# Two feed-forward matmuls merged into one of 512 columns, with one PSUM bank for each half of a slot

## The chip, the cores and the metric

The kernel runs on one core of a Trainium2 chip. The metric is the device time of one execution in microseconds (us). TensorE multiplies matrices into PSUM (8 banks of 128 x 512 float32), VectorE, ScalarE and GpSimd work on tiles in SBUF (GpSimd does not touch PSUM here), and the queue of SyncE starts the loads. In the rows the engines are called PE (matmuls), PEld (its weight loads), DVE (VectorE), ACT (ScalarE), POOL (GpSimd) and SPq.

## What is computed

A trunk of two layers over 256 tokens of width 1024. Each layer is a feed-forward, a token mixer of three branches, and another feed-forward:

```python
def _swiglu(h, w_in, w_out):
    gate, up = jnp.split(h @ w_in, 2, axis=-1)
    return (jax.nn.silu(gate) * up) @ w_out

for l in range(DEPTH):                      # 2
    mod = (c_act @ ada_w[l] + ada_b[l]).reshape(bsz, 3, 3, D_MODEL)
    h = _modulated_norm(x, norm_g[l, 0], mod[:, 0, 0], mod[:, 0, 1])
    x = x + MACARON_WEIGHT * mod[:, 0, 2][:, None, :] * _swiglu(h, ffn1_w_in[l], ffn1_w_out[l])
    ...                                     # token mixer
    h = _modulated_norm(x, norm_g[l, 2], mod[:, 2, 0], mod[:, 2, 1])
    x = x + MACARON_WEIGHT * mod[:, 2, 2][:, None, :] * _swiglu(h, ffn2_w_in[l], ffn2_w_out[l])
```

w_in is 1024 x 5632 (2816 gate and 2816 up columns), w_out 2816 x 1024, all float32.

## The kernel before

All weights stream through SBUF in slots of 128 x 2048, 100 slots a layer, four raw buffers and two rounded ones. Activations lie transposed: features on the partitions, the 256 tokens along the columns. Each product is made of three matmuls in a reduced float32 format: ScalarE rounds the raw weights (round_w, L561 to L568, tile wh), VectorE subtracts to get the remainder (split, L873 to L884, tile wl), and h is held as h_hi and h_lo in the same way. mm3 (L1406) then issues high weights by h_hi, high weights by h_lo, low weights by h_hi, 256 columns each, all added up in one place of a bank.

The first half of a feed-forward has 22 slots (KF, numbered j). A slot holds 128 gate and 128 up columns for all eight 128-row blocks of h. TensorE (ffn, L1489) does the gate half into columns 0 to 255 of bank j % 4 and the up half into columns 256 to 511 of the same bank (in_tile, L1423), 24 matmuls each. Slot 0 goes block by block as the norm delivers h (first_slot, L1412). At the start of slot j TensorE waits for hf of slot j - 4 (L1494).

When a slot's matmuls are done (w_used), ScalarE rounds the weights of slot j + 2 and takes the Silu of the gate half from PSUM (L602 to L607). VectorE splits slot j + 2 (L930), multiplies the up half in PSUM by the Silu into hf (L934), and then does one piece of the adaLN products (ada, L945 to L962): two instructions over 128 x 512, written ada below, the first of each group of four pieces a TENSOR_SCALAR. GpSimd turns hf into hid_hi (L1324) and hid_lo (L1326) for the second half of the feed-forward. Every fourth slot TensorE sums up a finished group of four ada pieces with four small matmuls (ada_sum, L1474 to L1481), issued behind slots 4, 8, 12, 16 and 20 of the first feed-forward of a layer and behind slots 8, 12, 16 and 20 of the second; the last piece it waits for is the one that VectorE does in the slot before. In the second feed-forward VectorE has ada pieces in slots 4 to 19 only.

The second half of the feed-forward (11 slots, row_slot, L1434) gathers its outputs in the four banks of OUT_BANKS (L151). Each engine works through its own queue in the order of the program; engines meet at semaphores whose counts are given per layer (PER_LAYER, L127), some with a start value (BEFORE, L149).

Of the kernel before, what the change touches and what calls it, by code (L numbers as in the profile page):

```python
# [29 lines left out]
P = 128  # L30
# [72 lines left out]
def shape_constants():  # L103
# [34 lines left out]
    "u_ready": 4, "gn_sub": 1, "gn_rinv": 1, "ya_final": 1, "ya_lo": 1, "mod_done":  # L138
    1, "br_used": 12, "merged": 4, "mg_lo": 4, "hid_ready": 44, "pb_zero": 1, "sb_min": 3,
    "shift_d": 12, "kk0": 1, "X_ready": 10, "vec_rows": 1, "w_used": 100,  # L140
# [9 lines left out]

OUT_BANKS = ((4, 5, 6, 2), (4, 5, 6, 7), (4, 5, 6, 2))  # L151
BR_BANKS = (0, 4, 0)
# [8 lines left out]
def hybrid_trunk(nc, a, per_layer, tally):  # L161
    out_dram = a["out"]
    ctx = ExitStack()
    with ctx:
# [24 lines left out]
        phase("h_gap", 64)  # L189
        hh = sb("h_hi", [P, KD, T], F32R)  # L190
        hl = sb("h_lo", [P, KD, T], F32R)
        scr = sb("scr", [P, KD, T])
# [52 lines left out]
        sil = v3(at_("sil", 2 * T), 2)  # L245
        hf = v3(at_("hf", 2 * T), 2)

        yh = v3(at_("y_hi", 9 * T, F32R, 0), 9)
# [69 lines left out]
        def bank(b):  # L318
            return PS[:, b, :]
# [240 lines left out]
        def _(act):  # L560
# [37 lines left out]
            def ffn(l, f):  # L598
                s0, s1 = (FFN1_IN, FFN1_OUT) if f == 0 else (FFN2_IN, FFN2_OUT)
                for s, o in steps(act, s0, KF):  # L600
                    j = s - s0
                    round_w(s + 2, o, l)  # L602
                    act.wait_ge(*at("w_used", s + 1 + o(4), l))

                    act.wait_ge(*at("hf_ready", f * KF + j - 1 + o(4), l))
                    nc.scalar.activation(sil[:, j % 2, :], PS[:, j % 4, 0:T], ACT.Silu)\
                        .then_inc(*one("sil_ready"))  # L607
                for s, o in steps(act, s1, 11, peel=1, tail=2):
                    if s < s1 + 9 or (s == s1 + 9 and f == 0):
                        round_w(s + 2, o, l)  # L610
# [259 lines left out]
        def _(dve):  # L870
# [55 lines left out]
            def ffn(l, f):  # L926
                s0, s1 = (FFN1_IN, FFN1_OUT) if f == 0 else (FFN2_IN, FFN2_OUT)
                for s, o in steps(dve, s0, KF, *((0, 0), (4, 2))[f]):
                    j = s - s0
                    split(s + 2, o, l)  # L930
                    dve.wait_ge(*at("sil_ready", f * KF + j + 1 + o(4), l))

                    dve.wait_ge(*at("hid_ready", f * KF + j - 1 + o(4), l))
                    V.tensor_tensor(hf[:, j % 2, :], PS[:, j % 4, T:2 * T], sil[:, j % 2, :], ALU.mult)\  # L934
                        .then_inc(*one("hf_ready"))
                    if f == 0 or 4 <= j < 20:
                        ada((16, 60)[f] + j, o, l)
                for s, o in steps(dve, s1, 11, peel=1, tail=2):
                    j = s - s1
                    if j < 9:  # L940
                        split(s + 2, o, l)
                    if 1 <= j <= 8:
                        ada((37, 79)[f] + j, o, l)
# [35 lines left out]

            for name in ("w_split", "hf_ready"):  # L980
                dve.sem_inc(sem(name), BEFORE[name])
            V.memset(epsb[:, :], EPS)
# [329 lines left out]
        def _(pool):  # L1312
            G = nc.gpsimd

            def ffn(l, f):
                s0 = FFN1_IN if f == 0 else FFN2_IN
                for s, o in steps(pool, s0, KF):
                    j = s - s0
                    pool.wait_ge(*at("hf_ready", f * KF + j + 1 + o(4), l))
                    dh = hidh[:, bass.ds(o(4) + j, 1), :].rearrange("p a b -> p (a b)")  # L1320
                    dl = hidl[:, bass.ds(o(4) + j, 1), :].rearrange("p a b -> p (a b)")

                    pool.sem_inc(sem("pool_on"), 1)
                    G.tensor_copy(dh, hf[:, j % 2, :])  # L1324
                    pool.drain()
                    G.tensor_tensor(dl, hf[:, j % 2, :], dh.bitcast(F32), ALU.subtract).then_inc(*one("hid_ready"))  # L1326

            pool.sem_inc(sem("hid_ready"), BEFORE["hid_ready"])

            r6 = slice(NOPE, P)  # L1330
# [72 lines left out]
        def _(pe):  # L1403
# [8 lines left out]
            def first_slot(s, b, h0, l):  # L1412
# [8 lines left out]
                return ins  # L1421

            def in_tile(s, half, b, col, n=P):  # L1423

                for k in range(KD):
                    w0 = (half * KD + k) * n
                    last = mm3(PS[0:n, b, col:col + T], (s % 2, slice(w0, w0 + n)), hh[:, k, :], hl[:, k, :],
                               k == 0, k == KD - 1)
                return last
# [59 lines left out]
            def ffn(l, f):  # L1489
                s0, s1 = (FFN1_IN, FFN1_OUT) if f == 0 else (FFN2_IN, FFN2_OUT)  # L1490
                for s, o in steps(pe, s0, KF, peel=(2, 6)[f]):
                    j = s - s0

                    pe.wait_ge(*at("hf_ready", f * KF + j - 3 + o(4), l))  # L1494
                    if j == 0:
                        ins = first_slot(s, 0, f * 2 * KD, l)
                    for half in range(2) if j else ():
                        split_ready(s, half, o, l)
                        ins = in_tile(s, half, j % 4, half * T)
                    ins.then_inc(*one("w_used"))  # L1500
# [4 lines left out]
                for s, o in steps(pe, s1, 11, *((1, 2), (2, 1))[f]):  # L1505
                    j = s - s1
                    pe.wait_ge(*at("hid_ready", f * KF + 2 * j + 2 + o(8), l))
                    if s == s1:

                        pe.wait_ge(*at("hid_ready", f * KF + 19, l))  # L1510

# [481 lines left out]
```

## Time and profile before

| | us |
|---|---|
| median of 3 runs | 1542.92 |
| lowest and highest | 1537.63, 1545.36 |
| the profiled execution | 1541.46 |
| its span, first to last instruction | 1539.7 |

The profiled execution is one of its own beside the three timed runs; all durations come from it. Its time stands 1.8 us over its span. A timeline row gives the start in us from the span's start, the duration in us, the engine, the line, the operation, what it writes and reads with their shapes, how many were merged into the row (x2), and in brackets how long the engine had been idle and what released it. TensorE's matmuls overlap one another: their pace is read from start to start, not from their durations.

### The profile page before, as it was taken

To read this page: it belongs to the slowest core of one execution; us is meant where nothing else is said; L and a number is where in the kernel's file an instruction comes from. 1 tells how busy PE (TensorE), PEld (TensorE's weight loads), DVE (VectorE), ACT (ScalarE), POOL (GpSimd) and SP (SyncE) were. 2 spreads that over 40 slices of the span, in tenths; PEclk is the share of its full clock that TensorE was granted. 3 is DMA by queue.
4 is the path that set the end of the run, shared out by engine and by line. 5 is a ranking of instruction groups with operands and counts; after the bars stand their busy time and mean duration, and the time that the engine had idled before them with its cause. 6 is when DMAs were issued, how large, how long until landed. Compare 5 with 4: busy or idle time off the path is not lost.

```text
span 1539.7 us, 31567 instructions
## 1 busy us (share of the span) xinstructions
PE 1401.4 (91%) x13297; PEld 1354.0 (88%) x13297; DVE 1009.5 (66%) x1327; ACT 652.2 (42%) x933; POOL 214.7 (14%) x250
## 2 busy tenths in 40 slices
PE   3699998978989998999989999897888999899997
PEld 3699998977779998999989999897777999899997
DVE  5777767656645776676677776765665468667655
ACT  2433434464533435334354333437373243543432
POOL 2133200021030000232003230002102000023200
PEclk9799999998999999999999999998999999999998
DMA  7998875923501856997669896792331095599860
GB/s 266 304 275 267 294 258 153 243 59 84 136 3 40 278 167 183 264 267 266 220 190 289 262 298 234 211 246 56 109 110 30 3 289 174 158 268 269 278 216 30
DMA packets 352798, 298.23 MB, mean 194 GB/s; under 512 B 19735, under 2 KB 295216, under 8 KB 352688
## 3 DMA queue, kind: packets, MB, share of 16 engines
q1 hardware_dynamic: 352688, 296.70, 64.5%
q8 instruction: 77, 1.26, 0.3%
q14 instruction: 33, 0.27, 0.1%
HBM read 295.61 MB, written 1.05 MB: 193 GB/s over the span
## 4 chain that ended last, share of the span: by engine, by line
PE 78%; DVE 10%; ACT 6%; DVEq 2%; issue 2%; DMA 2%; ACTq 1%; SPq 0%
PE PS L1408 21%; PE PS L1410 21%; PE PS L1409 21%; DVE ada_acc L961 3%; PE PS L1479 3%; ACT wh L567 2%; DVE wl L877 2%; PE PS L1825 2%; PE PS L1470 1%; DMA raw<-in_mix_w_in 1%; DVE PS L890 1%; DMA x_rows<-in_x 1%; PE PS L1816 1%; DVEq L948 1%; DVE scr L905 0%
## 5 line engine op out<-in xcount | busy, mean ns | idle before, releaser
L1408 PE MATMUL PS<-h_hi,wh 128*128 128x256 f32 x2256 | 645.4, 286 | 45.4 <-DVE h_lo L899 28.2
L567 ACT ACTIVATE wh<-raw 128x1024 fp32r<-128x1024 f32 (+1 forms) x400 | 396.0, 1038 | 607.9 <-PE PS L1410 583.0
L877 DVE TENSOR_TENSOR wl<-raw,wh 128x1024 fp32r<-128x1024 f32 (+1 forms) x400 | 473.6, 1225 | 270.2 <-ACT wh L567 270.2
L1409 PE MATMUL PS<-h_lo,wh 128*128 128x256 f32 x2256 | 637.8, 283 | 0.0
L1410 PE MATMUL PS<-h_hi,wl 128*128 128x256 f32 x2256 | 637.5, 283 | 0.0
L1408 PEld LDWEIGHTS PS<-h_hi,wh 128*128 128x128 f32 x2256 | 436.0, 193 | 51.3 <-issue 44.4
L1409 PEld LDWEIGHTS PS<-h_lo,wh 128*128 128x128 f32 x2256 | 437.1, 194 | 0.1
L1410 PEld LDWEIGHTS PS<-h_hi,wl 128*128 128x128 f32 x2256 | 436.6, 194 | 0.0
L961 DVE SCALAR_TENSOR_TENSOR ada_acc<-ada_w_ring,cact,ada_acc 128x512 f32<-128x512 f32 x280 | 219.4, 784 | 24.5 <-issue 1.8
L1408 PE MATMUL PS<-hid_hi,wh 128*128 (+1 forms) x704 | 197.7, 281 | 0.2
L1409 PE MATMUL PS<-hid_lo,wh 128*128 (+1 forms) x704 | 197.0, 280 | 0.0
L1410 PE MATMUL PS<-hid_hi,wl 128*128 (+1 forms) x704 | 197.0, 280 | 0.0
L1324 POOL CAST hid_hi<-hf 128x256 fp32r<-128x256 f32 x88 | 64.4, 732 | 728.3 <-DVE hf L934 728.3
L1409 PEld LDWEIGHTS PS<-hid_lo,wh 128*128 128x128 f32 x704 | 133.2, 189 | 0.0
L1410 PEld LDWEIGHTS PS<-hid_hi,wl 128*128 128x128 f32 x704 | 133.2, 189 | 0.0
L1408 PEld LDWEIGHTS PS<-hid_hi,wh 128*128 128x128 f32 x704 | 132.4, 188 | 0.3 <-issue 0.2
L1326 POOL TENSOR_TENSOR hid_lo<-hf,hid_hi 128x256 fp32r<-128x256 f32 x88 | 80.6, 916 | 12.7 <-issue 0.2
L1479 PEld LDWEIGHTS PS<-cst,ada_acc 128*128 128x128 f32 x320 | 41.3, 201 | 25.1 <-DVE ada_acc L961 17.6
L1479 PE MATMUL PS<-cst,ada_acc 128*128 128x1 f32 x320 | 43.0, 255 | 20.0 <-DVE ada_acc L961 19.6
L1383 POOL TENSOR_TENSOR rw_m<-scr 128x256 f32<-128x256 f32 x24 | 22.2, 944 | 158.4 <-ACT scr L659 86.9
L957 DVE TENSOR_SCALAR ada_acc<-ada_w_ring,cact 128x512 f32<-128x512 f32 x40 | 23.4, 585 | 30.2 <-PE PS L1479 16.9
L1398 POOL TENSOR_TENSOR A_X<-A_T,cst 128x384 f32<-128x384 f32 x20 | 23.4, 1172 | 135.1 <-DVE A_T L1189 109.1
(285 smaller groups left out, 1391.4 us busy)
## 6 DMA issues: line engine op xcount, KB each, us to landing
raw<-in_ffn_w_in SPq DMA_DIRECT2D x176, 512.0 KB, 5.4
ada_w_ring<-in_ada_w SPq DMA_DIRECT2D x160, 512.0 KB, 5.1
raw<-in_mix_w_in SPq DMA_DIRECT2D x90, 512.0 KB, 5.9
raw<-in_ffn_w_out SPq DMA_DIRECT2D x44, 1024.0 KB, 5.7
raw<-in_branch_w SPq DMA_DIRECT2D x8, 1024.0 KB, 8.2
raw<-in_mix_w_out SPq DMA_DIRECT2D x8, 1024.0 KB, 4.9
raw<-in_mix_w_in SPq DMA_DIRECT2D x2, 1024.0 KB, 7.5
w_mla<-in_mla_w_uq SPq DMA_DIRECT2D x4, 288.0 KB, 5.2
```

The costliest lines, as they stand in the source:

```text
L567: nc.scalar.activation(wh[:, s % 2, h * n:(h + 1) * n], raw[:, s % 4, h * n:(h + 1) * n], ACT.Copy).then_inc(*one("w_hi"))
L877: V.tensor_tensor(wl[:, s % 2, h * n:(h + 1) * n], raw[:, s % 4, h * n:(h + 1) * n], wh[:, s % 2, h * n:(h + 1) * n].bitcast(F32), ALU.sub ...
L957: V.tensor_scalar(acc[:, :], w, cc, None, ALU.mult)
L961: last = V.scalar_tensor_tensor(acc[:, :], w, cc, acc[:, :], ALU.mult, ALU.add)
L1324: G.tensor_copy(dh, hf[:, j % 2, :])
L1326: G.tensor_tensor(dl, hf[:, j % 2, :], dh.bitcast(F32), ALU.subtract).then_inc(*one("hid_ready"))
L1398: G.tensor_tensor(X[tt], AT[tt], chunk_mask(LEVELS[b]), ALU.mult).then_inc(*one("X_ready"))
L1408: M(out, wh[(slice(None),) + wsl], rhs_h, start=start, stop=False, skip_group_check=True)
L1409: M(out, wh[(slice(None),) + wsl], rhs_l, start=False, stop=False, skip_group_check=True)
L1410: return M(out, wl[(slice(None),) + wsl], rhs_h, start=False, stop=stop, skip_group_check=True)
L1479: ins = M(PS[:, 7, bass.ds(o(4) + col + i, 1)], acc[:, i * P:(i + 1) * P], onecol, start=True, stop=True)
L1825: ins = M(PS[half(q), b, o:o + 64], lhs[half(q), par, c, :], rhs[half(q), par, c, :], start=True, stop=True)
```

## The change

In the first half of both feed-forwards h_hi and h_lo now lie side by side for each block (tile h_both, of which hh and hl are views). The high weights meet both in one matmul of 512 columns, which fills a bank: columns 0 to 255 hold high by high, 256 to 511 high by low. The low weights meet h_hi in a second matmul of 256 columns into columns 0 to 255. Gate and up halves of a slot get a bank each, 2 * (j % 2) and the one after it. So TensorE waits at slot j for hf of slot j - 2.

ScalarE copies columns 256 to 511 of both banks to SBUF (gu), VectorE adds them to columns 0 to 255 (gu_sum), ScalarE takes the Silu of the gate sum from SBUF, and GpSimd, in place of VectorE, multiplies it by the up sum into hf, ahead of the two instructions it had. The second halves use bank 1 in place of bank 2.

```diff
-OUT_BANKS = ((4, 5, 6, 2), (4, 5, 6, 7), (4, 5, 6, 2))
+OUT_BANKS = ((4, 5, 6, 1), (4, 5, 6, 7), (4, 5, 6, 1))
...
-        hh = sb("h_hi", [P, KD, T], F32R)
-        hl = sb("h_lo", [P, KD, T], F32R)
+        both = sb("h_both", [P, KD, 2, T], F32R)
+        hh, hl = both[:, :, 0, :], both[:, :, 1, :]
...
+        gu = at_("gate_up", 4 * T)[:, :].rearrange("p (a b n) -> p a b n", a=2, b=2)
+        gu_sum = at_("gate_up_sum", 4 * T)[:, :].rearrange("p (a b n) -> p a b n", a=2, b=2)
...
# ScalarE, ffn
-                    nc.scalar.activation(sil[:, j % 2, :], PS[:, j % 4, 0:T], ACT.Silu)\
+                    for i in range(2):
+                        nc.scalar.activation(gu[:, j % 2, i, :], PS[:, 2 * (j % 2) + i, T:2 * T], ACT.Copy)\
+                            .then_inc(*one("gu_low"))
+                    act.wait_ge(*at("gu_ready", 2 * (f * KF + j) + 1, l))
+                    nc.scalar.activation(sil[:, j % 2, :], gu_sum[:, j % 2, 0, :], ACT.Silu)\
                         .then_inc(*one("sil_ready"))
...
# VectorE, ffn
                     split(s + 2, o, l)
-                    dve.wait_ge(*at("sil_ready", f * KF + j + 1 + o(4), l))
-
-                    dve.wait_ge(*at("hid_ready", f * KF + j - 1 + o(4), l))
-                    V.tensor_tensor(hf[:, j % 2, :], PS[:, j % 4, T:2 * T], sil[:, j % 2, :], ALU.mult)\
-                        .then_inc(*one("hf_ready"))
+                    dve.wait_ge(*at("hf_ready", f * KF + j - 1, l))
+                    for i in range(2):
+                        dve.wait_ge(*at("gu_low", 2 * (f * KF + j) + i + 1, l))
+                        V.tensor_tensor(gu_sum[:, j % 2, i, :], PS[:, 2 * (j % 2) + i, 0:T], gu[:, j % 2, i, :], ALU.add)\
+                            .then_inc(*one("gu_ready"))
...
# GpSimd, ffn
-                    pool.wait_ge(*at("hf_ready", f * KF + j + 1 + o(4), l))
+                    pool.wait_ge(*at("sil_ready", f * KF + j + 1, l))
+                    pool.wait_ge(*at("gu_ready", 2 * (f * KF + j) + 2, l))
...
+                    G.tensor_tensor(hf[:, j % 2, :], gu_sum[:, j % 2, 1, :], sil[:, j % 2, :], ALU.mult)\
+                        .then_inc(*one("hf_ready"))
+                    pool.drain()
                     G.tensor_copy(dh, hf[:, j % 2, :])
...
# TensorE
+            def both_halves(s, half, k, b, col, first, last):
+
+                w = (slice(None), s % 2, slice(col, col + P))
+                M(bank(b), wh[w], both[:, k, :, :].rearrange("p a b -> p (a b)"), start=first, stop=False,
+                  skip_group_check=True)
+                return M(PS[:, b, 0:T], wl[w], hh[:, k, :], start=False, stop=last, skip_group_check=True)
+
+            def wide_tile(s, half, b):
+                for k in range(KD):
+                    ins = both_halves(s, half, k, b, (half * KD + k) * P, k == 0, k == KD - 1)
+                return ins
...
-                    pe.wait_ge(*at("hf_ready", f * KF + j - 3 + o(4), l))
+                    pe.wait_ge(*at("hf_ready", f * KF + j - 1 + o(4), l))
                     if j == 0:
-                        ins = first_slot(s, 0, f * 2 * KD, l)
+                        ins = wide_first(s, f * 2 * KD, l)
                     for half in range(2) if j else ():
                         split_ready(s, half, o, l)
-                        ins = in_tile(s, half, j % 4, half * T)
+                        ins = wide_tile(s, half, 2 * (j % 2) + half)
...
-                        pe.wait_ge(*at("hid_ready", f * KF + 19, l))
+                        pe.wait_ge(*at("hf_ready", f * KF + 21, l))
```

wide_first does for slot 0 what wide_tile does, block by block as h comes. The start value of hf_ready is now set by GpSimd.

## Rows read from the trace of the kernel before

**Rows 1.** The page: busy time by engine; the chain that ended last, by engine.

```profile
PE 1401.4 (91%) x13297; PEld 1354.0 (88%) x13297; DVE 1009.5 (66%) x1327; ACT 652.2 (42%) x933; POOL 214.7 (14%) x250
...
PE 78%; DVE 10%; ACT 6%; DVEq 2%; issue 2%; DMA 2%; ACTq 1%; SPq 0%
```

**Rows 2.** Windows, one slot: busy us per engine, clock, DMA share, GB/s.

```profile
148.50:154.00 5.50, 5.50 (x49) 5.34 (x48) 4.26 (x6) 2.28 (x3) 2.02 (x3) 1.00 0.96 285
```

**Rows 3.** Timeline, TensorE: first and last of 192 matmuls (four slots).

```profile
132.01 0.36 PE L1408 MATMUL PS<-h_hi,wh 128*128 128x256 f32 x1
...
153.76 0.28 PE L1410 MATMUL PS<-h_hi,wl 128*128 128x256 f32 x1
```

**Rows 4.** Timeline, TensorE: first and last of 48 matmuls of 128 columns.

```profile
281.36 0.22 PE L1462 MATMUL PS<-wh,h_hi 128*128 128x128 f32 x1
...
286.55 0.28 PE L1464 MATMUL PS<-wl,h_hi 128*128 128x128 f32 x1
```

**Rows 5.** Timeline of one slot's steps: start us, us, engine, line.

```profile
148.69 2.01 ACT L567 ACTIVATE wh<-raw 128x1024 fp32r<-128x1024 f32 x2 [3.16 <-PE PS L1410]
150.61 0.36 ACT L606 ACTIVATE sil<-PS 128x256 f32<-128x256 f32 x1
...
149.79 2.36 DVE L877 TENSOR_TENSOR wl<-raw,wh 128x1024 fp32r<-128x1024 f32 x2 [1.07 <-ACT wh L567]
152.07 0.42 DVE L934 TENSOR_TENSOR hf<-PS,sil 128x256 f32<-128x256 f32 x1
152.58 1.58 DVE L961 SCALAR_TENSOR_TENSOR ada_acc<-ada_w_ring,cact,ada_acc 128x512 f32<-128x512 f32 x2
...
152.65 0.93 POOL L1324 CAST hid_hi<-hf 128x256 fp32r<-128x256 f32 x1 [3.34 <-DVE hf L934]
153.73 1.01 POOL L1326 TENSOR_TENSOR hid_lo<-hf,hid_hi 128x256 fp32r<-128x256 f32 x1
...
154.30 1.05 PE L1479 MATMUL PS<-cst,ada_acc 128*128 128x1 f32 x8 [0.26 <-DVE ada_acc L961]
155.21 0.36 PE L1408 MATMUL PS<-h_hi,wh 128*128 128x256 f32 x1
```

**Rows 6.** Timeline of the next slot (TENSOR_SCALAR first), and POOL beside an idle VectorE.

```profile
158.08 0.68 DVE L957 TENSOR_SCALAR ada_acc<-ada_w_ring,cact 128x512 f32<-128x512 f32 x1 [0.16 <-issue]
158.84 1.07 DVE L961 SCALAR_TENSOR_TENSOR ada_acc<-ada_w_ring,cact,ada_acc 128x512 f32<-128x512 f32 x1
...
158.08 0.40 POOL L1324 CAST hid_hi<-hf 128x256 fp32r<-128x256 f32 x1 [3.34 <-DVE hf L934]
158.63 0.74 POOL L1326 TENSOR_TENSOR hid_lo<-hf,hid_hi 128x256 fp32r<-128x256 f32 x1
...
612.13 0.73 POOL L1326 TENSOR_TENSOR hid_lo<-hf,hid_hi 128x256 fp32r<-128x256 f32 x1
```

**Rows 7.** Timeline: a weight split with POOL at work beside it.

```profile
319.77 3.43 DVE L877 TENSOR_TENSOR wl<-raw,wh 128x1024 fp32r<-128x1024 f32 x2
...
319.94 2.18 POOL L1376 TENSOR_TENSOR sb_z<-sb_z,cst 128x512 f32<-128x512 f32 x1 [1.66 <-DVE sb_s L1034]
```

**Rows 8.** Timeline, TensorE: where sums of the ada group start.

```profile
84.09 1.05 PE L1479 MATMUL PS<-cst,ada_acc 128*128 128x1 f32 x8 [0.27 <-DVE ada_acc L961]
...
107.90 1.05 PE L1479 MATMUL PS<-cst,ada_acc 128*128 128x1 f32 x8
...
131.10 1.05 PE L1479 MATMUL PS<-cst,ada_acc 128*128 128x1 f32 x8 [0.27 <-DVE ada_acc L961]
...
645.87 1.05 PE L1479 MATMUL PS<-cst,ada_acc 128*128 128x1 f32 x8 [0.26 <-DVE ada_acc L961]
```

**Rows 9.** Timeline, ScalarE: the first slot of the two feed-forwards of layer 0.

```profile
62.16 2.01 ACT L567 ACTIVATE wh<-raw 128x1024 fp32r<-128x1024 f32 x2 [4.28 <-PE PS L1410]
64.19 1.28 ACT L606 ACT_TABLE_LOAD   x1
...
602.19 2.01 ACT L567 ACTIVATE wh<-raw 128x1024 fp32r<-128x1024 f32 x2 [3.46 <-PE PS L1410]
```

More of the change, by code:

```diff
@@ L138 @@
     "u_ready": 4, "gn_sub": 1, "gn_rinv": 1, "ya_final": 1, "ya_lo": 1, "mod_done":
-    1, "br_used": 12, "merged": 4, "mg_lo": 4, "hid_ready": 44, "pb_zero": 1, "sb_min": 3,
+    1, "br_used": 12, "merged": 4, "mg_lo": 4, "hid_ready": 44, "gu_low": 88, "gu_ready": 88, "pb_zero": 1, "sb_min": 3,
     "shift_d": 12, "kk0": 1, "X_ready": 10, "vec_rows": 1, "w_used": 100,
@@ L977, in half_gate @@
                 return V.tensor_scalar(hgate[:, n, :], mod[:, (3 * n + 2) * KD:(3 * n + 3) * KD], w, None, ALU.mult)
-            for name in ("w_split", "hf_ready"):
-                dve.sem_inc(sem(name), BEFORE[name])
+            dve.sem_inc(sem("w_split"), BEFORE["w_split"])
             V.memset(epsb[:, :], EPS)
@@ L1328, in _ @@
             pool.sem_inc(sem("hid_ready"), BEFORE["hid_ready"])
+            pool.sem_inc(sem("hf_ready"), BEFORE["hf_ready"])
             r6 = slice(NOPE, P)
@@ L1421, in first_slot, with wide_first @@
                 return ins
+            def both_halves(s, half, k, b, col, first, last):
[7 more added lines that the diff above has]
+                return ins
+            def wide_first(s, h0, l):
+                split_ready(s, 1, still, l)
+                for k in range(KD):
+                    pe.wait_ge(*at("h_ready", h0 + k + 1, l))
+                    for half in range(2):
+                        ins = both_halves(s, half, k, half, (half * KD + k) * P, k == 0, k == KD - 1)
+                return ins
             def in_tile(s, half, b, col, n=P):
```

## The prediction, made before the change was run

> **What bounds the kernel now.** I read the page first: TensorE is busy 91% of the span and carries 78% of the chain that ended last [rows 1]. In a slot of a feed-forward's first half it works without a hole at granted clock 1.00, the 2.4 GHz level [rows 2]. So I asked what sets its pace. Four slots, 192 matmuls of 256 columns, start within 21.75 us, 113.3 ns apart but for the first step [rows 3]; a slot of 48 lasts L = 5.44 us. A matmul of 128 columns, half the streaming, follows its predecessor in 110.4 ns (5.19 us over 47 steps) [rows 4]. The pace hardly depends on the columns: what an instruction and its weight load cost each time sets it. That is where the change can win.
>
> Then I followed one slot through the other engines [rows 5]. Its matmuls end at E = 148.43: the next slot's last one starts at 153.76 [rows 3], plus 0.11, less 5.44. ScalarE's rounding starts at E + 0.26, VectorE's two splits end at E + 3.64 (152.07), hf runs to E + 4.06, the ada pair ends at E + 5.73 (154.16), and the ada sum starts on TensorE at E + 5.87 (154.30). The next slot's matmuls begin 0.91 later [rows 5] and lose another 0.09 on their first step, so 1.00. The ada sum is needed only every fourth slot, and there it, not TensorE, ends the wait: four slots take 3L + 5.87 + 1.00 = 23.19 us, and the trace has 131.10 to 154.30, 23.20 [rows 5, 8]. There is a longer kind, 84.09 to 107.90, 23.81 [rows 8], in which the matmuls are 117.8 ns apart (L = 5.65). Of the 14 such spans in the four feed-forwards, nine are short and five long: mean 23.41. GpSimd's result is not waited for today: a bank is used again four slots later.
>
> **Part 1, the matmuls.** Per slot, 16 triples of 256 columns become 16 pairs of 512 and 256. Columns are the same. The 256 part keeps its 113.3 ns. The wide part has no row: it can't stream under 2 x 106.7 = 213.3 ns at 2.4 GHz, and at worst costs two of today's, 226.6. I add to the column time what half the columns fail to save today, 113.3 - 110.4 = 2.9 ns [rows 3, 4], giving 216.2. L' = 16 x (216.2 + 113.3) = 5.27 us; bounds 16 x (213.3 + 110.4) = 5.18 and 5.44, or 5.65 at the long kind's pace. So at best 0.17 to 0.26 us of 5.44 are won in a slot, if nothing else is late.
>
> **Part 2, two banks a slot.** A slot now fills two of four banks, so TensorE waits at slot j for hf of slot j-2, where it waited for j-4. Everything from the end of slot n to hf(n) must fit in the one slot between. All of TensorE's next matmuls and weight loads are queued behind that wait. The steps, from E as above:
> - ScalarE: rounding as before, to about E + 2.2. Then two PSUM copies of 256 columns, 0.36 each by the Silu's row [rows 5], to about E + 2.9, under VectorE's splits: nothing, as long as the splits are later than that.
> - VectorE: splits to E + 3.64. First add 0.42 (the row of hf, same operands) to E + 4.06. Second add 0.42 to E + 4.48.
> - Silu from SBUF, from E + 4.09: 0.36, at most 0.5, beside the second add.
> - VectorE's ada pair starts 0.09 after its last PSUM step, GpSimd 0.16 after it [rows 5]. GpSimd now multiplies: two inputs, 256 columns, 0.73 to 0.74 us when VectorE is idle (the row of hid_lo) [rows 6].
>
> **Part 3, GpSimd beside VectorE.** In the rows the cast takes 0.40 us alone but 0.93 when the ada pair's first instruction started before it, and hid_lo 1.01 instead of 0.74 [rows 5, 6]. It ends 1.00 after that first instruction's start, so it was let in at 0.60. The other way round, an ada instruction that meets hid_lo already running takes 1.07, not 0.75 [rows 6]. They shut one another out. The Trainium skill, SBUF - State Buffer, section Who interferes with whom, has the same as a rule: whoever starts first holds a port pair they share, and the other is blocked for the whole instruction. It speaks against this change, which puts a third GpSimd instruction into this stretch; taken literally it would make the split below late by up to 0.74 rather than 0.40, some 6 us more.
>
> Priced from the rows: the first ada instruction starts at E + 4.57, the multiplication is let in at 5.17, ends at 5.91. TensorE starts 0.14 after its releaser [rows 5] and loses 0.09 on the first step: H = 6.1 us after E (5.6 where no ada pair blocks it, in the second feed-forwards' slots 0 to 3; 5.3 if it cost no more than a cast). H is over L' in each of these. The ada pair's second instruction meets the multiplication and ends 0.3 later; with the second add the ada sum moves from E + 5.87 to E + 6.59.
>
> After the multiplication come cast and hid_lo, to about E + 7.7 (today E + 6.3, 154.74). The next slot's split starts at E + L' + 1.36 = E + 6.6. Today it starts after GpSimd is done. From now on, where two slots follow without a stall, it meets hid_lo. A pair of splits with GpSimd beside it all the time took 3.43 instead of 2.36, against 2.2 us of GpSimd work and more [rows 5, 7]. For one 0.74 us instruction I take 0.40 (bounds 0 and 0.74). Then GpSimd itself is 0.40 later in that slot, and a third slot's split, though it comes after a stall (E + 6.10 + 1.36 = E + 7.5 against E + 8.1), meets it as well. So the ada sum, which hangs on such a slot, starts K = 6.99 after its E.
>
> **The sum.** Let a slot begin after an ada sum, at 0. The second begins at L' (two slots back was long ago), the third at L' + H, since it waits for hf of the first, which ended at L'. It ends at L' + H + L'. The sum hangs on its ada pair and starts K later (the fourth slot fits in between), and 1.00 after that the next slot begins. In all L' + H + L' + K + 1.00 = 10.54 + 6.10 + 6.99 + 1.00 = 24.63 us, where 23.41 stood. +1.22, fourteen times: +17.1.
> First feed-forward, slot 0 to its first sum: today 84.09 - 61.90 = 22.19 (61.90 is 62.16 less the 0.26) [rows 8, 9]. Now slot 0's Silu has a table load of 1.28 before it [rows 9], which the add holds back: hf(0) lets slot 2 start at 0.26 + 3.83 + 1.28 + 0.39 + 0.16 + 0.74 + 0.23 = 6.9. Slot 3 starts at 12.17, ends at 17.44, sum at 17.44 + 6.99 = 24.43. +2.24, twice: +4.5.
> Second feed-forward, eight slots to its first sum: today 645.87 - 601.93 = 43.94 [rows 8, 9]. Now slot 2 starts at 6.9, 4 at 12.17 + 5.6 = 17.8, 6 at 23.04 + 5.95 = 29.0, slot 7 at about 34.8, ends 40.1, sum at 47.1. +3.1, twice: +6.2.
> Last slot, 5.52 to 5.27, four times: -1.0.
> Everything else (norms, second halves, bank 1 in place of 2, the layout of h, at the first slot columns at the low clock) costs nothing: bank 1 was last read in slot 20, two slots before its new user. Total +26.8. The profiled execution took 1541.5, 1.5 under the median of 1542.9: 1541.5 + 26.8 = 1568.
>
> **The rivals.**
> (a) Nothing shuts out: the multiplication takes 0.74, splits aren't late, the table load comes ahead of the wait for the add. H = 5.6, K = 6.29; four slots 10.54 + 5.6 + 6.29 + 1.0 = 23.43, heads +0.9, last slots -1.0: 1542. For it: 0.73 in slots without ada [rows 6]. Against it: 0.93 and 1.01 wherever the ada pair runs [rows 5].
> (b) Half of it: the multiplication is blocked, the splits aren't late. K = 6.59: 24.23 for four slots, +11.5, heads +8.3, -1.0: 1560.
> (c) The wide matmul wins nothing (the change doesn't do what it says), with the stalls: L' = 5.44, four slots 24.97, +21.8, heads +12.8, -0.3: 1576. At 5.65, 1585.
> (d) Faster: GpSimd's path fits in a slot, H at most 5.2, and the wide matmul is at its bound, L' = 5.18. Then TensorE stalls at the ada sum alone: 3 x 5.18 + 6.29 + 1.0 = 22.83, -8.1; heads -3.5, last slots -1.4: 1528. The point is H = L': the multiplication would have to take 0.33 us or less, under the 0.40 of a cast [rows 6].
>
> **How the numbers follow.** The sum as it stands, with (b) as its weaker form: 0.62. (a) 0.15, (c) 0.13, (d) 0.08, the rest 0.02. Predicted 1568. The range leaves out (d) and what lies past (c): 1541 to 1580. About 0.5% is what a measurement of this kernel can tell from no change, 1535 to 1551: faster 0.08 (d), same 0.15 (a), slower 0.77.
>
> **What would show it.** In the changed trace: pairs of matmuls near 329 ns; TensorE idle 0.6 to 0.9 us at every second or third slot's start, released by GpSimd's hf, 1.6 at slot 2; hf on GpSimd over 1.2 us long beside the ada pair; the second ada instruction near 1.07; ada sums 24.6 apart; some split pairs near 2.8. If TensorE never waits for hf, or the sums are under 23.4 apart, the argument is wrong.

## The result and the profile after

| | before | after |
|---|---|---|
| median, us | 1542.95 (1537.63 to 1545.36, 4 runs) | 1576.54 (1574.55 to 1577.93, 4 runs) |
| the profiled execution (its span) | 1541.46 (1539.7) | 1577.93 (1576.1) |
| ratio to before, 95% interval | 1 | 1.0222 (1.0192 to 1.0251) |
| TensorE instructions of 128x1 to 128x512 | 13297 | 11889 |

The changed kernel is slower by 2.2%: 1568 was predicted, with 1541 to 1580 as the range. The time lies inside the range, 8.5 us above the forecast. The profiled executions differ by 36.5 us, from 1541.46 to 1577.93.

The page of the kernel after: busy time by engine, the chain by engine, and two groups (busy us, mean ns of one, idle time ahead of them with its releaser). The first two lines answer to [rows 1].

```profile
PE 1424.0 (90%) x11889; PEld 1298.8 (82%) x11889; DVE 1071.3 (68%) x1415; ACT 712.7 (45%) x1109; POOL 280.9 (18%) x338
...
PE 70%; DVE 12%; ACT 8%; issue 3%; DVEq 3%; DMA 2%; POOLq 1%; ACTq 1%; SPq 0%
...
L1437 PE MATMUL PS<-h_both,wh 128*128 128x512 f32 x1408 | 511.4, 405 | 24.4 <-DVE h_both L906 19.9
...
L1331 POOL TENSOR_TENSOR hf<-gate_up_sum,sil 128x256 f32<-128x256 f32 x88 | 89.6, 1018 | 688.3 <-ACT sil L613 688.3
```

TensorE runs 1408 matmuls fewer and is busy 23 us longer. Its share of the last chain falls from 78% to 70%; DVE, ACT and the queue of POOL take it over. So both were at work: the matmuls took no less time, and TensorE waits more.

The timeline of TensorE after: a whole stretch between two ada sums, against [rows 3, 5, 8]. "..." leaves out matmuls of the same pace. The last row is GpSimd's multiplication ahead of the first hole.

```profile
110.14 0.28 PE L1439 MATMUL PS<-h_both,wl 128*128 128x256 f32 x1
111.09 1.05 PE L1510 MATMUL PS<-cst,ada_acc 128*128 128x1 f32 x8 [0.67 <-DVE ada_acc L968]
112.00 0.48 PE L1437 MATMUL PS<-h_both,wh 128*128 128x512 f32 x1
...
117.37 0.40 PE L1437 MATMUL PS<-h_both,wh 128*128 128x512 f32 x1
...
117.72 0.40 PE L1437 MATMUL PS<-h_both,wh 128*128 128x512 f32 x1
...
123.26 0.28 PE L1439 MATMUL PS<-h_both,wl 128*128 128x256 f32 x1
123.68 0.50 PE L1437 MATMUL PS<-h_both,wh 128*128 128x512 f32 x1
...
129.30 0.28 PE L1439 MATMUL PS<-h_both,wl 128*128 128x256 f32 x1
129.69 0.50 PE L1437 MATMUL PS<-h_both,wh 128*128 128x512 f32 x1
...
136.27 0.27 PE L1510 MATMUL PS<-cst,ada_acc 128*128 128x1 f32 x1 [0.68 <-DVE ada_acc L968]
...
122.43 1.12 POOL L1331 TENSOR_TENSOR hf<-gate_up_sum,sil 128x256 f32<-128x256 f32 x1 [4.53 <-ACT sil L613]
```

Read it by starts. Inside a slot the pair repeats every 0.35 us (117.37 to 117.72), of which the wide matmul takes 0.234 and the narrow one 0.118. The next slot follows at once at 117.72. The third starts 0.42 after its predecessor's last matmul (123.26 to 123.68), the fourth 0.39 after (129.30 to 129.69), where 0.12 is the pace: holes of about 0.3 us, and the first step after each is 0.1 slower. These rows have no bracket, but hf is done at 123.55 (122.43 + 1.12), 0.13 before the first late start, about the 0.14 that TensorE keeps from its releaser in [rows 5]. From sum to sum it is 25.18 us. All 14 such spans of the four feed-forwards measure 25.17 to 25.22, where 23.20 and 23.81 stood [rows 8]: (25.19 - 23.41) x 14 = 24.9 of the 36.5 us.

The other engines in the same stretch, after, against [rows 5, 6] (timeline; the last slot before the sum at 111.09, whose steps begin at 104.50; E = 104.24).

```profile
104.50 2.01 ACT L570 ACTIVATE wh<-raw 128x1024 fp32r<-128x1024 f32 x2 [1.43 <-PE PS L1439]
...
105.60 2.70 DVE L884 TENSOR_TENSOR wl<-raw,wh 128x1024 fp32r<-128x1024 f32 x2 [0.66 <-ACT wh L570]
108.22 0.74 DVE L941 TENSOR_TENSOR gate_up_sum<-PS,gate_up 128x256 f32<-128x256 f32 x2
109.05 1.90 DVE L968 SCALAR_TENSOR_TENSOR ada_acc<-ada_w_ring,cact,ada_acc 128x512 f32<-128x512 f32 x2
...
105.34 0.74 POOL L1336 TENSOR_TENSOR hid_lo<-hf,hid_hi 128x256 fp32r<-128x256 f32 x1
109.28 1.12 POOL L1331 TENSOR_TENSOR hf<-gate_up_sum,sil 128x256 f32<-128x256 f32 x1 [3.20 <-ACT sil L613]
```

The split pair ends later because hid_lo of the slot before (105.34 to 106.08) runs beside it: 2.70 instead of 2.36. The ada pair takes 1.90 instead of 1.58, hf 1.12 where GpSimd took 0.73 for the like beside an idle VectorE [rows 6]. By its instructions hf takes 733 ns at least, 1117 in the median, 1125 at most.

### The profile page after: what moved, and what is told of

It is laid out like the page before. It is cut to its first block, busy times and chain, and to the rows that moved or that the text cites. A ratio compares the mean times of both kernels' runs of the same rounds, so it can differ in the third digit from the quotient of the medians.

```text
span 1576.1 us, 29191 instructions
## 1 busy us (share of the span) xinstructions
PE 1424.0 (90%) x11889; PEld 1298.8 (82%) x11889; DVE 1071.3 (68%) x1415; ACT 712.7 (45%) x1109; POOL 280.9 (18%) x338
## 4 chain that ended last, share of the span: by engine, by line
PE 70%; DVE 12%; ACT 8%; issue 3%; DVEq 3%; DMA 2%; POOLq 1%; ACTq 1%; SPq 0%
PE PS L1437 14%; PE PS L1419 12%; PE PS L1420 11%; PE PS L1421 11%; PE PS L1439 7%; ACT wh L570 4%; DVE ada_acc L968 3%; DVE wl L884 3%; PE PS L1510 2%; PE PS L1856 2%; DVEq L955 2%; PE PS L1501 1%; POOLq L1333 1%; DMA raw<-in_mix_w_in 1%; DVE PS L897 1%
## 5 line engine op out<-in xcount | busy, mean ns | idle before, releaser
L884 DVE TENSOR_TENSOR wl<-raw,wh 128x1024 fp32r<-128x1024 f32 (+1 forms) x400 | 493.8, 1274 | 243.3 <-ACT wh L570 243.3
L1437 PE MATMUL PS<-h_both,wh 128*128 128x512 f32 x1408 | 511.4, 405 | 24.4 <-DVE h_both L906 19.9
L1439 PE MATMUL PS<-h_both,wl 128*128 128x256 f32 x1408 | 398.1, 283 | 0.0
L1437 PEld LDWEIGHTS PS<-h_both,wh 128*128 128x128 f32 x1408 | 267.8, 190 | 101.5 <-issue 38.3
L1419 PE MATMUL PS<-h_both,wh 128*128 128x256 f32 x848 | 248.3, 293 | 25.4 <-DVE h_both L906 8.3
L1439 PEld LDWEIGHTS PS<-h_both,wl 128*128 128x128 f32 x1408 | 267.5, 190 | 0.0
L968 DVE SCALAR_TENSOR_TENSOR ada_acc<-ada_w_ring,cact,ada_acc 128x512 f32<-128x512 f32 x280 | 236.1, 843 | 23.4 <-issue 0.5
L1420 PE MATMUL PS<-h_both,wh 128*128 128x256 f32 x848 | 242.9, 286 | 0.0
L1421 PE MATMUL PS<-h_both,wl 128*128 128x256 f32 x848 | 242.7, 286 | 0.0
L1331 POOL TENSOR_TENSOR hf<-gate_up_sum,sil 128x256 f32<-128x256 f32 x88 | 89.6, 1018 | 688.3 <-ACT sil L613 688.3
L1419 PEld LDWEIGHTS PS<-h_both,wh 128*128 128x128 f32 x848 | 166.8, 197 | 30.0 <-issue 23.0
L1420 PEld LDWEIGHTS PS<-h_both,wh 128*128 128x128 f32 x848 | 167.5, 198 | 0.1
L1421 PEld LDWEIGHTS PS<-h_both,wl 128*128 128x128 f32 x848 | 166.5, 196 | 0.0
L613 ACT ACTIVATE sil<-gate_up_sum 128x256 f32<-128x256 f32 x88 | 36.8, 418 | 126.1 <-DVE gate_up_sum L941 126.1
```

The costliest lines, as they stand in the source:

```text
L613: nc.scalar.activation(sil[:, j % 2, :], gu_sum[:, j % 2, 0, :], ACT.Silu)\
L884: V.tensor_tensor(wl[:, s % 2, h * n:(h + 1) * n], raw[:, s % 4, h * n:(h + 1) * n], wh[:, s % 2, h * n:(h + 1) * n].bitcast(F32), ALU.sub ...
L968: last = V.scalar_tensor_tensor(acc[:, :], w, cc, acc[:, :], ALU.mult, ALU.add)
L1331: G.tensor_tensor(hf[:, j % 2, :], gu_sum[:, j % 2, 1, :], sil[:, j % 2, :], ALU.mult)\
L1419: M(out, wh[(slice(None),) + wsl], rhs_h, start=start, stop=False, skip_group_check=True)
L1420: M(out, wh[(slice(None),) + wsl], rhs_l, start=False, stop=False, skip_group_check=True)
```

## Experiments

Each kernel was timed beside the kernel before on one chip. The medians of before in the three series are 1542.74, 1540.84 and 1542.26 us; the ratios below are to those. "Sums" are the starts of successive ada sums on TensorE, 14 spans in a run.

**One wide matmul or two narrow ones.** The changed kernel, its 512-column matmul issued as two of 256, all else as changed:

```diff
-                M(bank(b), wh[w], both[:, k, :, :].rearrange("p a b -> p (a b)"), start=first, stop=False, ...)
+                M(PS[:, b, 0:T], wh[w], hh[:, k, :], start=first, stop=False, ...)
+                M(PS[:, b, T:2 * T], wh[w], hl[:, k, :], start=False, stop=False, ...)
```

> The changed kernel with its 512-column matmul issued as two of 256 columns (48 matmuls and weight loads a slot again, into the same banks); all else as changed. Theory 1: the wide matmul costs by its columns (234 ns, twice 117), the weight loads it saves were hidden anyway; then the time stays within 5 us of the changed kernel's 1577, the ada sums 25.2 us apart. Rival (the prediction's): every instruction with its load costs some 10 ns of its own; then a slot is 0.17 us longer and the kernel 8 us slower, 1585. Third: narrow matmuls get back to 113.3 ns in part of the slots, as in the kernel before; then it is faster by up to 8 us, 1569.

Measured: 1575.59 us (1572.80 to 1576.08), ratio 1.021 (1.0178 to 1.0243), sums 24.97 to 25.00 apart in 8 spans and 25.17 to 25.18 in 6. Timeline of TensorE, narrow kernel:

```profile
119.83 0.28 PE L1438 MATMUL PS<-h_both,wh 128*128 128x256 f32 x1
...
120.73 0.28 PE L1437 MATMUL PS<-h_both,wh 128*128 128x256 f32 x1
```

The rows shown are the first and the ninth matmul: eight steps in 0.90 us, 113 ns each, so that three take 0.34 against 0.35 for the wide pair. About half of the triples in these spans take 0.34, the others 0.35. The first theory holds, and in part the third: the wide matmul saves nothing; a 512-column matmul costs two of 256 at the slower of the two paces that before shows. The whole gain that the change was to pay with is absent.

**Multiplication back on VectorE.** Here hf is computed by VectorE from the sums, after the adds and ahead of the ada pair; GpSimd casts and subtracts as before (the waits that go with it are left out of the diff):

```diff
+                    V.tensor_tensor(hf[:, j % 2, :], gu_sum[:, j % 2, 1, :], sil[:, j % 2, :], ALU.mult)...
                     if f == 0 or 4 <= j < 20:
                         ada((16, 60)[f] + j, o, l)
...
-                    G.tensor_tensor(hf[:, j % 2, :], gu_sum[:, j % 2, 1, :], sil[:, j % 2, :], ALU.mult)...
```

> The changed kernel with the multiplication into hf moved back from GpSimd to VectorE, behind the two adds; GpSimd has its two instructions of before. Theory: GpSimd's blocked multiplication (1.12 us) is what makes hf later than a slot (6.0 to 6.3 us after the slot's end against 5.64), so with 0.42 us on VectorE hf is ready after about 5.3 us, TensorE doesn't wait for it, splits return to 2.36, the ada sum comes about 6.75 after its slot's end: 24.7 us between sums, 12 us faster in all, 1565. Rival: the matmuls alone make the loss and the stalls are covered by something else; then 1577 stays.

Measured: 1584.09 us (1581.38 to 1588.01), ratio 1.0276 (1.0241 to 1.031): 7.5 us above the changed kernel's median, where 12 us less or no change had been expected. The holes at the starts of slots are gone. Seven of the 14 spans are 24.89 to 25.02, the other seven 26.39 to 26.44. The windows around one of the latter (the sum starts at 108.68; busy us of each engine with the number of instructions, granted clock, DMA share, GB/s):

```profile
108.70:111.00 2.30, 2.30 (x16) 2.09 (x17) 2.28 (x2) 1.48 (x3) 0.42 (x1) 0.98 1.18 319
111.00:114.50 3.50, 3.50 (x13) 3.02 (x12) 3.09 (x6) 0.42 (x1) 1.13 (x2) 0.53 0.79 249
114.50:118.00 3.50, 3.50 (x22) 3.04 (x21) 0.08 (x1) 0.90 (x1) 0.00 (x0) 1.00 1.03 301
```

and two wide matmuls of the same stretch (timeline, TensorE):

```profile
111.20 0.63 PE L1437 MATMUL PS<-h_both,wh 128*128 128x512 f32 x1
...
111.84 0.63 PE L1437 MATMUL PS<-h_both,wh 128*128 128x512 f32 x1
```

TensorE stood still from its last matmul of the slot (107.26) to the sum, 1.42 us. Some 2.3 us after the sum's start the granted clock falls to 0.53 in the mean of a window, the 1.2 GHz level for most of it; the pair takes 0.64 us (111.20 to 111.84) instead of 0.35. Five such pairs cost 5 x 0.29 = 1.5 us, the difference of the two kinds of span. K is 6.96 here (E = 101.72), as late as in the changed kernel: three slots without a hole, 1.00 + 3 x 5.64 + 6.96 = 24.88, are all that moving the multiplication saves, 0.3 us of 25.19. TensorE comes to the sum earlier and waits longer, and the seven slow stretches cost more than the 14 x 0.3 us.

**A third pair of banks.** The changed kernel with pairs of banks taken in turn by j % 3 and TensorE waiting for hf of slot j-3 (TensorE's loop over the slots is written out for it, and the second halves go back to bank 2):

```diff
-                    pe.wait_ge(*at("hf_ready", f * KF + j - 1 + o(4), l))
+                    pe.wait_ge(*at("hf_ready", f * KF + j - 2 + o(4), l))
...
-                        ins = wide_tile(s, half, 2 * (j % 2) + half)
+                        ins = wide_tile(s, half, 2 * (j % 3) + half)
```

> The changed kernel with three pairs of banks instead of two (TensorE's loop over the slots written out), so that it waits for hf of slot j - 3; GpSimd's work stays. Theory: the stalls at slot starts (0.3 us each) and 1.3 us at slot 2 go, the ada sum still ends each four slots: 3 x 5.64 + 6.9 + 1.0 = 24.8 us between sums instead of 25.2, 10 us faster in all, 1567. Rival: the wait moves to the splits or the sum and nothing is won, 1577.

Measured: 1582.96 us (1580.99 to 1588.55), ratio 1.0258 (1.0226 to 1.0291), where 10 us less or no change had been expected. The pattern is that of the kernel before it: six spans of 24.90 to 24.92, eight of 26.41 to 26.47. With no stall at the slots, GpSimd's work and the splits lie on one another. Timeline of this kernel, VectorE, GpSimd, TensorE:

```profile
104.98 2.91 DVE L884 TENSOR_TENSOR wl<-raw,wh 128x1024 fp32r<-128x1024 f32 x2 [0.28 <-ACT wh L570]
...
105.10 1.71 POOL L1336 TENSOR_TENSOR hid_lo<-hf,hid_hi 128x256 fp32r<-128x256 f32 x1
...
109.16 0.28 PE L1439 MATMUL PS<-h_both,wl 128*128 128x256 f32 x1
110.59 1.05 PE L1510 MATMUL PS<-cst,ada_acc 128*128 128x1 f32 x8 [1.15 <-DVE ada_acc L968]
```

Two engines that meet cost each other 0.55 us (split) and 0.97 us (hid_lo) here. And the idle time ahead of the sum is 1.43 us again.

**Is it the idle time that lowers the clock?** The kernel with the multiplication on VectorE, and eight matmuls of 256 columns ahead of every ada sum, into a bank that nobody reads then; they are work that the reference doesn't ask for:

```diff
+                        for _ in range(8):
+                            M(PS[:, 6, 0:T], hh[:, 0, 0:P], hh[:, 0, :], start=True, stop=True)
                         ada_sum((3, 14)[f] + j // 4, l, o)
```

> a_dve with eight matmuls of 256 columns, whose result nobody reads, ahead of every ada sum, so that TensorE works through most of the 1.4 us that it waits there for VectorE. Theory: a_dve (1584) is slower than the changed kernel only because in about half of its spans the granted clock falls to half for some 3 us after this idle stretch (24.9 us between sums where it does not fall, 26.4 where it does); with the stretch filled all spans take 24.9 and the kernel 1584 - 9 x 1.5 = 1570. Rival: the clock falls for another reason; then 1584 and the spans of 26.4 stay.

Measured: 1573.27 us (1565.17 to 1575.98, 5 runs), ratio 1.021 (1.0175 to 1.0245). All 14 spans are 24.88 to 25.02. Timeline of TensorE and one window of this kernel:

```profile
109.14 1.12 PE L1534 MATMUL PS<-h_both 128*128 128x256 f32 x8
110.45 1.05 PE L1510 MATMUL PS<-cst,ada_acc 128*128 128x1 f32 x8 [0.19 <-DVE ada_acc L972]
...
111.00:114.50 3.50, 3.50 (x22) 3.09 (x22) 3.21 (x5) 1.37 (x4) 0.00 (x0) 1.00 0.90 274
```

Work that nobody needs makes the kernel faster, by the medians 10.8 us (1584.09 to 1573.27), about 7 x 1.5; by the ratios 0.0066, about 10 us. The clock stays at 1.00. The mean granted clock of the executions says the same: 0.951 to 0.959 in the four without the eight matmuls, 0.960 to 0.966 in the five with them. So the slow stretches came from TensorE standing still ahead of the sum.

**Taking the wait at the sum away.** The ada sum is moved into the middle of the next slot, after its first half, where the ada pair is long done:

```diff
                         ins = wide_tile(s, half, 2 * (j % 2) + half)
+                        if half == 0 and j % 4 == 1 and j >= (5, 9)[f]:
+                            ada_sum((3, 14)[f] + j // 4, l, o)
```

The old place is removed. The edit was made in the changed kernel, in the one with the third pair of banks, in the one with the multiplication on VectorE, and in the kernel before, the last with in_tile in place of wide_tile.

> The changed kernel with each ada sum issued between the halves of the next slot; the multiplication stays on GpSimd and the banks stay two pairs. Theory: the wait for the ada pair goes, the waits for hf stay: two slots take 5.64 + 6.1, four 23.5 to 24.1 us instead of 25.2, about 1560. Rival: only the wait for hf counts and the sum was hidden behind it; then 1577.

> Three pairs of banks and the ada sum between the halves: no wait of TensorE for hf of two slots back or for the ada pair; GpSimd still multiplies. Theory: what is left is VectorE and GpSimd shutting each other out (splits of 2.9 us instead of 2.36, ada pairs of 1.9 instead of 1.6), 5.7 to 5.8 us of VectorE a slot, 23.6 to 24.0 us in four, about 1552. Rival: with TensorE never idle they fit into 5.64 and the time is that of a_dve_mid or better.

> a_dve (multiplication on VectorE) with each ada sum issued between the halves of the next slot, so that TensorE has neither a wait for hf nor one for the ada pair, and no idle stretch after which its clock is lower. Theory: both losses of the changed kernel are these waits; four slots take 4 x 5.64 + 0.95 = 23.5 us, the whole about 1548 (the table load still delays slot 2). Rival: VectorE, with 2.4 + 0.75 + 0.43 + 1.6 us and the gaps between them in a slot of 5.64, becomes the bound, 24.2 us and 1558 or more.

> The kernel before with each ada sum of the feed-forwards' first halves issued between the two halves of the next slot instead of ahead of it. Theory: the sum's wait for VectorE's ada pair (0.43 us over the end of the slot) goes; four slots take 4 x 5.44 + 0.95 = 22.7 instead of 23.2, eighteen times: 8 us faster than before, 1535. Rival: VectorE's next group of ada pieces now waits for the later sum and gives it back, 1543.

| the sum in the middle, in | us, median | ratio (interval) | sums apart, us |
|---|---|---|---|
| the changed kernel | 1564.91 (1564.18 to 1572.30) | 1.0175 (1.0135 to 1.0216) | 24.61 to 24.65 |
| with three pairs of banks | 1546.99 (1541.41 to 1551.58) | 1.0040 (1.0018 to 1.0062) | 23.50 |
| with the multiplication on VectorE | 1545.17 (1539.66 to 1548.96) | 1.0030 (1.0012 to 1.0048) | 23.50 |
| the kernel before | 1542.34 (1533.83 to 1546.14) | 0.9996 (0.9975 to 1.0017) | 23.50 to 23.51 |

In the changed kernel the wait for hf remains, and costs more than was expected of it (1565, not 1560). Timeline of TensorE, starts of two successive slots:

```profile
95.93 0.28 PE L1439 MATMUL PS<-h_both,wl 128*128 128x256 f32 x1
96.34 0.49 PE L1437 MATMUL PS<-h_both,wh 128*128 128x512 f32 x1
...
101.97 0.28 PE L1439 MATMUL PS<-h_both,wl 128*128 128x256 f32 x1
102.36 0.49 PE L1437 MATMUL PS<-h_both,wh 128*128 128x512 f32 x1
```

A slot takes 6.02 us, 0.37 more than the 5.65 of its matmuls. The slot with the sum has 0.90 of its own and hides the wait: 3 x 6.02 + 5.65 + 0.90 = 24.61. With the wait for hf gone as well, in either way, the span is 4 x 5.65 + 0.90 = 23.50, TensorE has no hole in it, and 4 to 6 us over before are left. The two waits together are all the rest of the loss. The kernel with three pairs of banks had been expected to stay slower for its meetings of VectorE and GpSimd; they are still there (2.94 us for a split pair, up to 1.71 for hid_lo), and cost nothing in the spans once TensorE waits for neither. The timeline of TensorE in the kernel with the multiplication on VectorE, and in before with the sum moved (its first sum):

```profile
110.29 0.95 PE L1510 MATMUL PS<-cst,ada_acc 128*128 128x1 f32 x8
```

```profile
80.01 0.28 PE L1410 MATMUL PS<-h_hi,wl 128*128 128x256 f32 x1
...
83.41 0.28 PE L1410 MATMUL PS<-h_hi,wl 128*128 128x256 f32 x1
83.53 0.95 PE L1479 MATMUL PS<-cst,ada_acc 128*128 128x1 f32 x8
...
84.65 0.28 PE L1410 MATMUL PS<-h_hi,wl 128*128 128x256 f32 x1
...
86.77 0.28 PE L1410 MATMUL PS<-h_hi,wl 128*128 128x256 f32 x1
```

Neither row of the sum has a bracket: nothing is waited for. In before this wins nothing, because all matmuls of the 14 spans now run at the long pace of 117.8 ns: 4 x 5.65 + 0.90 = 23.5 in every span, where before had 23.20 in nine spans and 23.81 in five. The rival's 1543 came, but not by its mechanism: VectorE waits for the sums no longer than in before (15.5 us in the whole execution, 16.9 before). Nor is it enough to say that matmuls without a stop run at the long pace. In the rows above 30 steps from 80.01 to 83.41 take 113.3 ns each, as do all from 60.1 us on, without a stop; behind the sum, for which TensorE did not wait either, 18 steps from 84.65 to 86.77 take 117.8.

**Another way to shorten the wait of before.** The kernel before with the ada pair ahead of the split on VectorE:

```diff
+                    if f == 0 or 4 <= j < 20:
+                        ada((16, 60)[f] + j, o, l)
                     split(s + 2, o, l)
```

> The kernel before with VectorE's ada piece of each slot put ahead of its weight split, into the 1.07 us in which it waits for ScalarE, so that the ada sum never waits. Theory: four slots take 4 L + 0.95; at the pace of 113.3 ns a matmul that is 22.7 us instead of 23.4 on average and the kernel is 8 to 10 us faster, 1533. Rival: as in b_mid, matmuls that never stop at a sum run at 117.8 ns (L = 5.65), 23.5 us, and nothing is won, 1543.

Measured: 1542.46 us (1536.55 to 1552.65, 12 runs), ratio 1.0013 (0.999 to 1.0036), spans 23.50 to 23.51, all at the long pace. It ends where the moved sum did, as its rival said.

**What a narrow matmul costs.** The changed kernel with its 512 columns cut unequally, another cut in each feed-forward: 448+64, 384+128, 320+192 and four of 128. It was run once.

```diff
+                cuts[0] = ((448,), (384,), (320,), (128, 256, 384))[2 * l + f]
```

> The changed kernel with the 512-column matmul cut in another way in each of the four feed-forwards, all columns still computed: 448 + 64, then 384 + 128, then 320 + 192, then four of 128. Read from start to start inside a slot. Theory 1 (price by column, 0.458 ns each, with a floor of some 110 ns from the weight load): 205, 176 and 147 ns for 448, 384 and 320 columns, 110 for 64, 128 and 192. Rival (the prediction's term: 2.4 GHz column time and 2.9 ns a piece): 190, 163 and 136 ns. Theory 1 also says that the first three cuts cost a slot 16 x about 80 ns more than the wide matmul.

Timeline of TensorE, stretches of the four feed-forwards (a row x2 stands for the two pieces, a row x4 for the four):

```profile
99.68 0.40 PE L1442 MATMUL PS<-h_both,wh 128*128 128x448 f32 x2
99.92 0.36 PE L1445 MATMUL PS<-h_both,wl 128*128 128x256 f32 x1
100.11 0.40 PE L1442 MATMUL PS<-h_both,wh 128*128 128x448 f32 x2
...
639.79 0.40 PE L1442 MATMUL PS<-h_both,wh 128*128 128x384 f32 x2
...
640.19 0.39 PE L1442 MATMUL PS<-h_both,wh 128*128 128x384 f32 x2
...
859.70 0.40 PE L1442 MATMUL PS<-h_both,wh 128*128 128x320 f32 x2
859.94 0.30 PE L1445 MATMUL PS<-h_both,wl 128*128 128x256 f32 x1
...
860.84 0.40 PE L1442 MATMUL PS<-h_both,wh 128*128 128x320 f32 x2
...
1450.29 0.95 PE L1442 MATMUL PS<-h_both,wh 128*128 128x128 f32 x4
...
1451.36 0.95 PE L1442 MATMUL PS<-h_both,wh 128*128 128x128 f32 x4
```

The same 768 columns take 0.433, 0.403 and 0.380 us in the first three (the last is three rounds in 1.14 us, 859.70 to 860.84), against 0.353 in one wide and one narrow matmul: extra 80, 50 and 27 ns. Columns at the pace of the wide matmul cost 234.6 / 512 = 0.458 ns each, so 64, 128 and 192 columns would take 29, 59 and 88 ns; if none of them can take less than the 110.4 ns of [rows 4], the extras would be 81, 52 and 22. All three fit within 5 ns; the 80 ns that the expectation gave for every cut was its own slip. The rows also show where the time goes. From the first piece to the 256-column matmul it is 0.23 to 0.24 us, the price of 512 columns, whatever the cut; the lost time comes in the step behind that, 0.19 (99.92 to 100.11) where 0.12 is the pace. So the rival's 2.4 GHz column time falls, and what the small piece costs is a floor under its turn, not a price paid beside the columns: a matmul of 256 columns (117 ns of columns) is already above it. That the floor is the time of the weight load, as the expectation has it, no run shows. The fourth feed-forward, at 1.07 us, can't be read with the others, since it ran at the low clock; see the last section. The kernel took 1854.72 us.

## Why the prediction was right, and where it was not

- **L', the time of a slot's matmuls: the step that failed.** Predicted 5.27, with 5.44 and 5.65 as the upper bounds; measured 5.64 to 5.65, 16 pairs of 0.353 where the sign was 0.329. The prediction read from 110.4 ns for 128 columns beside 113.3 for 256 [rows 3, 4] that an instruction has a fixed price and that its columns are nearly free, and gave the wide matmul 213.3 + 2.9 ns. The runs show a floor of about 110 ns and a column price of 0.443 to 0.460 ns, which happen to meet near 256 columns. The wide matmul is all columns: 234.6 ns, not 216.2. This term alone is 2 x 0.37 = 0.74 us of a four-slot span. It is the mechanism of rival (c), which had a chance of 0.13. The number is right because the range reached as far as that rival; the gain that the change was to bring, 0.17 us a slot, did not come.
- **The same term by the Trainium skill.** The Trainium skill, TensorE: Matmul & The Clock Gate, section Wait — 56ns, not 53.3ns?, puts back-to-back matmuls at the full clock at columns / 2.4 GHz plus some 2.5 ns, which makes an estimate of 215.8 ns for 512 columns. The trace disagrees: 234 to 235 ns at granted clock 1.00; the measurement decides. The section does not say whether its matmuls had this number format and a weight load each, as these have. Its formula gives nearly the size that the prediction had formed from rows, and both were short by 18 to 19 ns.
- **H, the wait for hf: right.** Predicted 6.1 us from the end of slot n to a full-speed slot n+2; measured 123.68 - 117.73 = 5.95, plus 0.09 on the first step, 6.04. Since L' is longer than predicted, the hole is 0.3 us and not 0.6 to 0.9. The sign "hf over 1.2 us beside the ada pair" was a little high: 1.12.
- **K, from E to the ada sum: right.** Predicted 6.99; measured 111.09 - 104.24 = 6.85, where 5.87 stood. Its parts: the second add and the blocked ada pair, and the split behind hid_lo, 0.34 of the 0.40 taken. The rule of the Trainium skill, SBUF - State Buffer, section Who interferes with whom, taken literally, asked up to 0.74 for that split; the trace stays below it here: the two overlap for 0.48 us (105.60 to 106.08), and the split lost 0.34. With the third pair of banks, where they overlap by more, the split lost 0.55.
- **The span.** 1.00 + 5.64 + 6.04 + 5.64 + 6.85 = 25.17; measured 25.17 to 25.22; predicted 24.63. Two terms of -0.06 and -0.14 stand against +0.74. Over 14 spans the miss is 24.9 - 17.1 = 7.8 us, nearly all of the 9.7 us by which the profiled execution passed the sum of 26.8.
- **The heads (from the end of slot 0 to the first ada sum): right in sum, by luck, since two errors cancel.** 85.92 - 61.55 = 24.37 (predicted 24.43) and 655.24 - 608.25 = 46.99 (predicted 47.1). But the predicted idle time of 1.6 us at slot 2 isn't there: its first matmul starts at 67.31, 5.76 after the end of slot 0, not 6.9. The table load was predicted to stand behind the wait for the add. Timeline of ScalarE and VectorE in that slot, after:

```profile
64.38 1.28 ACT L613 ACT_TABLE_LOAD   x1
65.18 0.75 DVE L941 TENSOR_TENSOR gate_up_sum<-PS,gate_up 128x256 f32<-128x256 f32 x2
65.67 0.42 ACT L613 ACTIVATE sil<-gate_up_sum 128x256 f32<-128x256 f32 x1
```

  The load starts at 64.38, 0.80 before the add that the Silu waits for, and is over at 65.66, where the add was done by about 65.59. It costs 0.07 here. The longer L' gave back what this saved.
- **Last slots and the rest.** -1.0 was predicted for the four last slots, from the shorter L'; with 5.64 nothing is won. All that lies outside spans and heads changed by 36.5 - 24.9 - 2 x (2.18 + 3.05) = +1.1 us in sum, as +3.9 and -2.9 between single feed-forwards. It was not taken apart.
- **The rivals.** (a) falls: hf takes 1.12 where the ada pair runs, and the splits are late; only its third part, the table load ahead of the wait for the add, is what happened. (b) falls with the late splits. (d) needed hf under 0.33 us. (c) with its 5.44 gave 1576, and the median is 1576.5; but with the measured 5.64 it would have given nearly 1585. It was met by 5.64 together with a smaller H and K and no stall for the table load.
- **What each half of the change costs.** The matmul's width is worth nothing (narrow against wide, 1575.6 and 1576.5). The waits are worth nearly everything: with both gone the kernel is at 1545, 1547. What is left there, 4 to 6 us, is 0.3 to 0.4% and clear of noise. The pace of the matmuls is of that size: in before the 4 and 8 slots ahead of the first sums all run at 113.3 ns, so 24 slots are 5.65 instead of 5.44, 5.0 us, and the 14 spans are 23.50 instead of 23.41, 1.3 us. No run takes that pace away, so this is worked out, not shown.

No kernel of these is faster than the one before.

## What to carry to other kernels

Before fusing two matmuls into a wider one, find two widths in the trace and ask whether the narrower shows a floor or a price per instruction: only a price is saved by fusing, and a pace near the floor looks like one. When work is moved to a second engine to free the first, count the stretches in which the two now meet and the number of slots that the result may be late; and if a chain feeds TensorE at one point only, moving that point by half a slot takes the chain off the path, as long as the chain is late by less than that; here it was late by 6.85 - 5.64 = 1.2 us against half a slot of 2.8.

## What the runs showed of the hardware

- **Idle time and the clock.** In the kernel after, TensorE stands still 0.95 us (start of the last matmul to start of the sum, 110.14 to 111.09) before each ada sum, and in all 14 spans the clock stays at 1.00. After stops of 1.42 us, counted in the same way, the clock fell in 15 of 28 spans (7 of 14 with the multiplication on VectorE, 8 of 14 with three pairs of banks, there every second time within a feed-forward), for some 3 us, and in the stretch shown it began to fall only 2.2 us after the sum's start. With matmuls in the gap it never fell in them. What decides between the 15 and the 13 was not found.
- **A stream of 128-column matmuls at the low clock.** Two windows of the kernel with the unequal cuts, one over the last feed-forward's first half and one behind it:

```profile
1389.30:1774.90 385.60, 385.55 (x1807) 385.58 (x1808) 100.20 (x132) 68.67 (x116) 48.24 (x63) 0.50 0.30 87
1775.00:1780.00 5.00, 5.00 (x46) 5.00 (x45) 1.20 (x3) 1.41 (x3) 1.87 (x3) 1.00 0.63 210
```

  TensorE is busy almost without a hole (385.55 of 385.60 us), and the granted clock is 0.50, the 1.2 GHz level, from the start of the 128-column matmuls at 1389.35 to their end (their last round starts at 1770.72) and 3 us into the 256-column matmuls behind them; then it rises. A round of 768 columns took 1.07 us, of which 640 ns are the columns at 1.2 GHz. Ahead of the low level TensorE had stopped for 4.17 us. Over the first halves with the first three cuts the clock is 0.97 to 1.00, and the kernel after, with a stop of 4.16 us at the same place, has 1.00 again from 1362 us on. It was seen in one run.
- **Two paces at one clock.** Matmuls of 256 columns run 113.3 or 117.8 ns apart, both at granted clock 1.00. Behind an ada sum for which TensorE had waited the spans of before ran at the short pace in 9 of 14 cases; behind one for which it had not waited it was 117.8 in all 28 (before with the sum moved, and with the ada pair ahead of the split). Ahead of the first sum of each feed-forward all matmuls of before run at 113.3, without a stop. With the sum moved this is so in three of the four, and the pace changes at that first sum, as in the rows shown above; in the fourth it is the long one from the start. The 512-column matmul showed 234 to 235 ns alone, twice the longer. So a removed wait can win nothing: that is what happened to before with its sum moved. What sets the kind stays open.
